# A hybrid attention and mLSTM block: where the identity matrix comes from, the order of the first loads, the place of the key transposes, and the order of some weight and activation forms

## The reference

```python
h = rms_norm(x, g_mix)
p = h @ w_in                       # columns: aq, ak, av, mq, mk, mv, mo, mi, mf
att = sliding_window_attention(rms_norm(aq), rms_norm(ak), av, sinks, slopes)   # 8 heads on 2 key heads
mq, mk = split(silu(causal_dwconv(concat(mq, mk))))
mh  = sigmoid(mo) * mlstm_chunkwise(mq, mk, mv, i_pre=mi, f_pre=mf)             # 4 heads
x = x + concat(rms_norm(att, g_att), rms_norm(mh, g_ml)) @ w_out
h2 = rms_norm(x, g_ffn)
x = x + (silu(h2 @ w_gate) * (h2 @ w_up)) @ w_down                              # D_FF = 2816
```

## Time and profile before

| | us |
|---|---|
| three timed runs | 1024.15, 1022.7, 1023.62 (median 1023.62) |
| the profiled execution, its own time | 1022.94 |
| its span, first to last instruction | 1021.1 |

### The profile page before, as it was taken

One profiled execution on the slowest core, in us unless ns is written; L12 is line 12 of the kernel. 1 busy time (PEld: TensorE's weight loads), 2 busy tenths in 40 slices (PEclk: granted clock), 3 DMA queues, 4 the chain that ended last, 5 costly groups with the idle time before them and its releaser, 6 DMA issues.

```text
span 1021.1 us, 13479 instructions
## 1 busy us (share of the span) xinstructions
PE 1005.1 (98%) x4970; PEld 831.3 (81%) x4970; DVE 646.9 (63%) x775; ACT 442.5 (43%) x912; POOL 691.5 (68%) x543
## 2 busy tenths in 40 slices
PE   9999999999999999999999999999999999999998
PEld 7898788877877887778888888888888888888886
DVE  4259426648862579584857676574848676574585
ACT  7555135547840558433434252433434252433440
POOL 0128768826566514988778688688778688688792
PEclk9999999999999999999999999999999999999999
DMA  7213202140131002111211211211211211211213
GB/s 228 68 53 91 77 28 67 60 154 22 32 110 57 25 18 82 52 42 42 83 42 42 83 42 42 82 42 42 83 42 42 83 42 42 83 41 43 84 58 136
DMA packets 71161, 66.06 MB, mean 65 GB/s; under 512 B 5304, under 2 KB 53688, under 8 KB 71096
## 3 DMA queue, kind: packets, MB, share of 16 engines
q1 hardware_dynamic: 70104, 64.71, 20.4%
q10 hardware_dynamic: 992, 0.49, 0.2%
HBM read 60.48 MB, written 4.21 MB: 63 GB/s over the span
## 4 chain that ended last, share of the span: by engine, by line
PE 91%; DVE 4%; issue 2%; ACT 2%; POOL 1%; DMA 0%; SPq 0%; DVEq 0%; POOLq 0%; ACTq 0%
PE banks L795 29%; PE banks L797 28%; PE banks L796 28%; PE banks L815 1%; ACT prob L1489 1%; PE banks L989 1%; PE banks L886 1%; DVE af_lo L2030 1%; PE banks L964 1%; POOL wr_raw L725 0%; PE banks L898 0%; DMA w_raw<-in_w_in 0%; PE banks L953 0%; PE banks L908 0%; PE banks L862 0%
## 5 line engine op out<-in xcount | busy, mean ns | idle before, releaser
L731 POOL TENSOR_TENSOR wr_lo<-wr_raw,wr_hi 128x512 fp32r<-128x512 f32 x231 | 318.8, 1412 | 26.8 <-ACT wr_hi L1309 21.7
L725 POOL TENSOR_TENSOR wr_raw<-wr_raw,wr_raw 128x512 f32<-128x512 f32 x132 | 193.8, 1473 | 138.0 <-PE banks L797 105.9
L795 PE MATMUL banks<-hf_hi,wr_hi 128*128 128x512 f32 x616 | 240.8, 391 | 1.8 <-DVE sg L2006 1.1
L797 PE MATMUL banks<-hf_hi,wr_lo 128*128 128x512 f32 x616 | 240.4, 390 | 0.0
L796 PE MATMUL banks<-hf_lo,wr_hi 128*128 128x512 f32 x616 | 240.1, 390 | 0.0
L1309 ACT ACTIVATE wr_hi<-wr_raw 128x512 fp32r<-128x512 f32 x231 | 136.7, 625 | 158.9 <-POOL wr_raw L725 100.4
L2109 DVE TENSOR_TENSOR x<-banks,x 128x1024 f32<-128x1024 f32 x138 | 168.8, 1224 | 53.3 <-PE banks L797 39.4
L795 PE MATMUL banks<-w_hi,actT_hi 128*128 128x512 f32 (+1 forms) x448 | 173.3, 387 | 0.9 <-DVE w_lo L1700 0.9
L797 PE MATMUL banks<-w_hi,actT_lo 128*128 128x512 f32 (+1 forms) x448 | 168.2, 376 | 0.0
L796 PE MATMUL banks<-w_lo,actT_hi 128*128 128x512 f32 (+1 forms) x448 | 167.8, 375 | 0.0
L795 PEld LDWEIGHTS banks<-hf_hi,wr_hi 128*128 128x128 f32 x616 | 115.6, 188 | 27.4 <-DVE sg L2006 2.0
(11 more groups left out here) (202 smaller groups left out, 1197.0 us busy)
## 6 DMA issues: line engine op xcount, KB each, us to landing
wr_raw<-in_w_up SPq DMA_DIRECT2D x46, 256.0 KB, 3.3
wr_raw<-in_w_gate SPq DMA_DIRECT2D x44, 256.0 KB, 3.4
wr_raw<-in_w_down SPq DMA_DIRECT2D x44, 256.0 KB, 3.1
w_raw<-in_w_in SPq DMA_DIRECT2D x32, 256.0 KB, 3.5
w_raw<-in_w_out SPq DMA_DIRECT2D x16, 256.0 KB, 2.7
x<-in_x SPq DMA_DIRECT2D x8, 512.0 KB, 6.4
out<-x SPq DMA_DIRECT2D x16, 256.0 KB, 2.1
x_in<-in_x SPq DMA_DIRECT2D x7, 512.0 KB, 4.0
```

The lines of the kernel that those rows point to most:

```text
L725: nc.gpsimd.tensor_tensor(wr_raw[slot(q, f)][:, :], wr_raw[slot(q, a)][:, :], wr_raw[slot(q, b)][:, :], ALU.subtract).then_inc(wsum, 1)
L731: nc.gpsimd.tensor_tensor(wr_lo[s][:, :], wr_raw[s][:, :], wr_hi[s][:, :].bitcast(F32), ALU.subtract).then_inc(wf_lo, 1)
L795: nc.tensor.matmul(ps, x_hi, wh, start=first, stop=False, skip_group_check=more)
L797: return nc.tensor.matmul(ps, x_lo, wh, start=False, stop=last, skip_group_check=more)
```

## The change

In seven places:

1. `ident` is not loaded any more. GpSimd makes it from the tile of ones with two `affine_select` instructions of 128x128, and TensorE waits for `ident_set`.
2. SP issues the first half of x first, then weight block 0, then the second half of x, then the other blocks; `grow` is issued by ScalarE. TensorE warms with 4 and 2 matmuls in place of 6 and 5, and transposes `grow` ahead of the tile. ScalarE does weight blocks 0 to 2 ahead of `high_bank(0, 1)` (before 0 and 1), VectorE blocks 0 to 3 ahead of `low_bank(0, 1)` (before 0 and 1).
3. `lf` is made before the keys are scaled; TensorE sums it after unit 18, and transposes the keys a unit later, after `u`; the copies to `kT` move with them.
4. On GpSimd, up 0's weight (q = 1): sums 5, 6, 4, then low part 6, then sum 7 and the other low parts; before: sums 5, 6, 7, 4 and then all low parts. The counts that ScalarE's `weight_high` waits for follow.
5. On VectorE in `first_gate_up`, `form_low(4)` is cut into two halves, and the add that frees the bank of gate 0 stands between them; TensorE waits for the second half only at its third k.
6. On VectorE in gate 1 (j = 1), the low part of form 3 moves behind the first add on bank 4, beside that of form 4.
7. The constants lose the identity's columns.

```diff
-            sp.dma_start(ident[:, :], consts[:, C_ID:C_ID + P]).then_inc(ident_s, 16)
             sp.dma_start(x_in[0][:, 0:N], x_t[0][:, 0:N]).then_inc(x_half_s, 16)
-            sp.dma_start(x_in[0][:, N:D], x_t[0][:, N:D]).then_inc(x_in_s[0], 16)
-            sp.dma_start(grow[:, :], g_mix.rearrange("a (k p) -> (a k) p", p=P)).then_inc(gmix_s, 16)
             for k in range(K):
                 sp.dma_start(w0_raw[:, k, :], w_in_k[k, :, MQ:MQ + N]).then_inc(w0_s[k], 16)
+                if k == 0:
+                    sp.dma_start(x_in[0][:, N:D], x_t[0][:, N:D]).then_inc(x_in_s[0], 16)
...
+            pool.wait_ge(ones_set, 1)
+            nc.gpsimd.affine_select(out=ident[:, :], in_=ones[:, :], pattern=[[1, P]], compare_op=ALU.is_ge,
+                                    fill=0.0, base=0, channel_multiplier=-1).then_inc(ident_lower, 1)
+            pool.wait_ge(ident_lower, 1)
+            nc.gpsimd.affine_select(out=ident[:, :], in_=ident[:, :], pattern=[[-1, P]], compare_op=ALU.is_ge,
+                                    fill=0.0, base=0, channel_multiplier=1).then_inc(ident_set, 1)
...
             pe.wait_ge(ones_set, 1)
-            keep_warm(6)
-            pe.wait_ge(ident_s, 16)
-            transpose_tile(x_in, 0, h_tp)
+            keep_warm(4)
+            pe.wait_ge(ident_set, 1)
             pe.wait_ge(gmix_s, 16)
             nc.tensor.transpose(bank[4][:, 0:K], grow[:, :], ident[0:K, 0:K]).then_inc(mix_tp, 1)
-            keep_warm(5)
+            transpose_tile(x_in, 0, h_tp)
+            keep_warm(2)
...
                 if U == 2 * T + 2:
-                    pe.wait_ge(kn_ready, 1)
-                    for b in range(2):
-                        for j in range(4):
-                            last = nc.tensor.transpose(bank[2 + b][:, j * P:(j + 1) * P],
-                                                       kvs[:, 4 * b + j, 2 * MH:2 * MH + KV * HD], ident[:, :])
-                    last.then_inc(kT_tp, 1)
-
                     pe.wait_ge(lf_ready, 1)
...
                 if U == 2 * T + 3:
                     pe.wait_ge(u_ready, 1)
                     nc.tensor.transpose(bank[6][0:32, 0:P], u_col[:, :], ident[:, :]).then_inc(uT_tp, 1)
+                    pe.wait_ge(kn_ready, 1)
+                    (the same eight transposes)
...
+            act.dma_start(grow[:, :], g_mix.rearrange("a (k p) -> (a k) p", p=P)).then_inc(gmix_s, 16)
             nc.scalar.preload_act_table_set("natural_log_exp_and_others")
             high_bank(0, 0, h_tp, h_hi)
             act.wait_ge(mix_ready, 1)
-            w0_high(0)
-            w0_high(1)
+            for k in range(3):
+                w0_high(k)
             high_bank(0, 1, h_tp, h_hi)
...
             low_bank(0, 0, h_hi, h_split)
-            w0_low(0)
-            w0_low(1)
+            for k in range(4):
+                w0_low(k)
             low_bank(0, 1, h_hi, h_split)
...
                     block_sum(q, 5, 7, 5)
+                    pool.wait_ge(wsum, sum_count(q, 5))
+                    pool.wait_ge(b22_s[q % 2], n)
+                    block_sum(q, 6, 3, 5)
+                    pool.wait_ge(wsum, sum_count(q, 6))
+                    pool.wait_ge(b21_again, 16)
+                    block_sum(q, 4, 4, 6)
+                    pool.wait_ge(wsum, sum_count(q, 4))
+                    block_low(q, 6)
+                    block_sum(q, 7, 3, 7)
+                    pool.wait_ge(wsum, sum_count(q, 7))
+                    for f in FORMS[3:]:
+                        block_low(q, f)
...
-                half_product(gate, 0, 4, False)
+                half_product(gate, 0, 4, False, second_half=8)
...
+                early = len(FORMS) - (2 if j == 1 else 1)
                 if j >= 1:
-                    for f in FORMS[1:-1]:
+                    for f in FORMS[1:early]:
                         act_low(j - 1, f)
                 dve.wait_ge(copied, 3 * g + 3)
                 add_product(sg[4], bank[4], 7 * g + 5)
                 if j >= 1:
-                    act_low(j - 1, FORMS[-1])
+                    for f in FORMS[early:]:
+                        act_low(j - 1, f)
...
-                form_low(4, slice(0, 4 * P), 7)
+                form_low(4, slice(0, 4 * P), 7, slice(0, 2))
                 dve.wait_ge(copied, copy_of(0, 2))
                 add_product(sg[4], bank[4], product(0, 7))
+                form_low(4, slice(0, 4 * P), 7, slice(2, 4))
```

More of the change, by code:

```diff
@@ L761, in _ @@
                     block_low(q, 2)
-                pool.wait_ge(wsum, 4 * q + 4)
-                for f in FORMS[2:]:
-                    block_low(q, f)
+                    for f in FORMS[2:]:
+                        block_low(q, f)
             for q in (QA, QB):
@@ L1060, in _ @@
                     nc.tensor.transpose(bank[6][0:32, 0:P], u_col[:, :], ident[:, :]).then_inc(uT_tp, 1)
+                    pe.wait_ge(kn_ready, 1)
+                    for b in range(2):
+                        for j in range(4):
+                            last = nc.tensor.transpose(bank[2 + b][:, j * P:(j + 1) * P],
+                                                       kvs[:, 4 * b + j, 2 * MH:2 * MH + KV * HD], ident[:, :])
+                    last.then_inc(kT_tp, 1)
                 if U == 2 * T + 4:
@@ L1107, in half_product @@
                 for k in range(4):
+                    if k == 2 and second_half:
+                        pe.wait_ge(h2_flo, second_half)
                     if k == 2 and tile is not None:
@@ L1329, in _ @@
             act.wait_ge(mix_ready, 1)
-            w0_high(0)
-            w0_high(1)
+            for k in range(3):
+                w0_high(k)
             high_bank(0, 1, h_tp, h_hi)
-            for k in range(2, K):
+            for k in range(3, K):
                 w0_high(k)
@@ L1710, in _ @@
             low_bank(0, 0, h_hi, h_split)
-            w0_low(0)
-            w0_low(1)
+            for k in range(4):
+                w0_low(k)
             low_bank(0, 1, h_hi, h_split)
-            for k in range(2, K):
+            for k in range(4, K):
                 w0_low(k)
@@ L1777, in _ @@
                 if U == 2 * T + 1:
+                    dve.wait_ge(softplus_done, 1)
+                    V_.scalar_tensor_tensor(lf[:, :].rearrange("p (t h) -> p t h", h=MH), fpre, 0.0,
+                                            expf[:, :].rearrange("p (t h) -> p t h", h=MH),
+                                            ALU.min, ALU.subtract).then_inc(lf_ready, 1)
                     dve.wait_ge(kv_rs, 1)
@@ L1807, in _ @@
                     V_.tensor_scalar(diag[:, :], tril32, cm[:, P - 1:P], None, ALU.mult).then_inc(umax_ready, 1)
+                    dve.wait_ge(kT_tp, 1)
+                    for b in range(2):
+                        step(V_.tensor_scalar(kT[:, CHUNK + b * N:CHUNK + (b + 1) * N], bank[2 + b][:, :],
+                                              cols[:, G_K:G_K + 1], None, ALU.mult))
                 if U == 2 * T + 4:
```

35 lines of the change are left out of this document (12 added, 23 removed).

## The result

| | before | after |
|---|---|---|
| timed runs, four each | 1022.70 to 1025.51, median 1023.88 | 1017.39 to 1018.04, median 1017.79 |
| ratio | | 0.9939, 95% interval 0.9922 to 0.9956 |
| the profiled execution, its own time | 1022.94 | 1017.68 |
| its span | 1021.1 | 1016.0 |

The change makes the kernel 0.6% faster. The runs of before spread over 2.8 us, those of after over 0.65; the experiments show that this is part of the result. The two profiled executions differ by 5.26 us, the forecast's terms made 3.9.

A forecast was written before the change was run, and what follows sets the result against it. TensorE, busy 1005.1 of 1021.1 us, was taken as the bound. Gains 1.45 + 0.95 + 1.0 + 0.5 = 3.9 took 1022.94 to 1019.0, or 1019.7 with the median's offset; predicted 1019.5, range 1017.9 to 1021.4.

The forecast's parts named there:

- the signs under "right": No TensorE idle over 0.2 at lf, seam forms 4 and 6, gate 1's form 4; affine_select by 3 us; unit 1 0.5 earlier.
- A pause costs the idle time shown plus 0.16: Price of each TensorE pause, from 512-column matmuls that start 0.23 us apart and show 0.39 each; four pauses, together 3.79.
- Keys: After unit 18 TensorE asks only for lf, ready near 102.7, and transposes the keys later: gain 1.45 us, bounds 1.0 and 1.53.
- Seam: Waits before 405.20 and 408.91 go, 0.44 + 0.81, less 0.3 given back by ScalarE's queue: gain 0.95, bounds 0.3 and 1.25.
- Rival 1: Seam: ScalarE's high part 7 waits for a late sum 7 and gives the 0.95 back: 1020.4 us; chance 0.13.
- Gate 1: A low part moves behind the add, which ends near 438.7, wanted at 439.39: gain 1.0 us, bounds 0.5 and 1.01.
- Start: Loads are issued earlier and the identity is hidden behind x: gain 0.5 us, bounds 0 and 0.83.
- the end of unit 0 follows those: Start: ScalarE takes the last three weight blocks as they land, so those landings set when unit 0 ends.
- Rival 2: The start gains nothing because transfers pace the landings: 1020.0 us; chance 0.08.
- rival 4: GpSimd's first affine_select is late and holds up unit 0; 4 us beyond 1.2 of free delay gives 1023; chance 0.06.
- Rival 5: TensorE's clock rises late at the start, 5.5 us a unit at half clock, two whole units low: 1027 us; chance 0.04.
- Rival 3: After unit 18, lf is late behind GpSimd by 0.5 or more: 1020.0 to 1020.4 us; chance 0.06.

The follow-up runs named there:

- the second measurement: The whole change measured once more on one chip beside a version with further edits: median 1018.19 us at full clock, ratio 0.9948 to the kernel before.
- keys_only: Only item 3 (lf made first, key transposes a unit later) put into the kernel before: 1021.22 us at full clock against 1022.88, ratio 0.9979.
- seam_only: Only items 4 and 5 (GpSimd's order for up 0, VectorE's form 4 cut) put into the kernel before: 1022.73 us at full clock against 1022.88, ratio 0.9997.
- start_only: Only items 1, 2 and 7 (identity on GpSimd, orders at the start) put into the kernel before: 1021.96 us at full clock against 1022.88, ratio 0.9991.
- grow_only: The kernel before with only the load of `grow` moved to ScalarE's queue: 1022.36 us at full clock against 1022.88, ratio 0.9991.
- gate_late: The kernel before, with form 4's low part in gate 1 also put ahead of the add on bank 4: 1024.17 us at full clock, ratio 1.0029.

## Why the prediction was off

**The direction and the mechanism of the keys, the seam and gate 1 were right; the sizes, the base and the start's path were not.** Pauses of TensorE were removed, and most of the gain came there. Of the signs under "right", 0.25 of idle stays at form 4 of gate 1, and unit 1 came 0.9 and not 0.5 earlier. The miss of 1.7 is 0.5 of base and 1.3 of terms that were priced too low or not at all, less 0.1 by which the median stands above the profiled execution. The upper bounds of the four terms add up to 4.6 (1.53, 1.25, 1.01, 0.83), below the 5.26 measured, so no choice within them would have met it. That the time lies outside the range at all is a matter of a tenth: the second measurement, 1018.19, lies inside.

**The base.** The forecast took the profiled execution's 1022.94 less 3.9, and moved up from 1019.0 to 1019.5 because the median of the timed runs stood higher. That half microsecond went the wrong way: 23 of 87 runs of before have the lower mean clock and are 2.7 above the others, and none of 70 with item 6 has it. So these runs do not remain as an offset, they are part of the gain. The prediction named this drift itself among the places where it fails most easily.

**"A pause costs the idle time shown plus 0.16"** was too little: the step behind the first matmul is 0.12 longer too. With 0.28 for each pause (0.24 for the one before 408.91, where the next step is 0.31) the rows of before give 1.66 for the keys (1.38 of idle), 1.45 for the seam (0.28 and 0.65) and, with 0.25 of idle left, 0.60 for gate 1: the measured 1.71, 1.48 and 0.61.

**Keys: 1.45 forecast, 1.71 measured, 1.66 in the runs of keys_only.** The mechanism is as written, and only the pause's price was off.

**Seam: 0.95 forecast, 1.48 measured in the whole change, 1.28 on top of gate 1's order.** The step that failed is the 0.3 that ScalarE's queue was to give back. High part 7 came about as late as forecast: it starts at 405.50, which with the 3.1 gained ahead of the seam is 408.6 on the clock of before, for 408.8. But from there to the copy ScalarE took 3.62, where the forecast had 4.0 (4.22 less 0.2 of pause), and the copy was done 0.3 before form 7. Rival 1 did not come.

**Gate 1: 1.0 forecast, 0.61 measured.** The step that failed is that the add ends near 438.7 and TensorE wants it at 439.39, with 0.7 of cover. Both times are from the timeline of before. With the seam's 0.95, by the forecast's own sum, TensorE wants it 0.95 earlier, and if VectorE's chain stays the cover is -0.25 and not 0.7. On the clock of before (3.1 added) TensorE wanted it at 437.9, 1.5 earlier than forecast, and the add ended at 438.3, only 0.4 earlier; the trace shows 0.25 of idle, and that it is the same figure is luck. The same slip in the reasoning hid the larger fact: the seam's term was worth next to nothing without gate 1's, as seam_only shows. The prediction added terms that were not independent, and was saved by the fact that both were in the change.

**Start: 0.5 forecast, 0.92 measured between the two profiles and in start_only's runs at full clock.** The bound was 0.83. The step that failed is "the end of unit 0 follows those", the landings. In the change's own profile no row of TensorE in unit 0 waits for a weight block, and the last low part ends 0.31 ahead of its matmul; in start_only's it is 1.26. What is earlier is unit 0's first matmul: 7.50 in the mean of the five profiles with the change's start, 8.47 in the seven with the old one, and slow steps have taken the place of waits. How the 0.92 is made up stays open. The last landing did move, by 1.3 in the mean of the profiles, more than the issues (0.83); 0.5 to 0.8 of that is `grow`, by one profile each. The forecast weighed the Trainium skill's page "Trainium Kernel Development and Optimization", section Key Constraints, by which issuing from a second queue saves issue time only, and took it to speak for less. In grow_only the last block landed 0.8 earlier than the mean of the old start for an issue 0.4 earlier; one profile against a spread of 1.0, so the rule is not refuted, but it gave no reason to shade the term. Rival 2 (nothing) falls. So does rival 4: the first `affine_select` began at 1.17 and took 0.29. The six microseconds of the Trainium skill's page "GPSIMD Engine Reference", section Instruction dispatch, do not show here; no row says whether its code was freshly loaded. (By the rival's own terms they would have cost 6 less 1.2, which is 4.8 and not some 4.)

**Rival 5, the clock at the start, came in part.** It was given 0.04 as a loss of several microseconds over whole units. It came as three slow steps here and up to nine in other profiles of the change's start, 0.2 each; in start_only the last of them ends at 11.45, so its sign, 0.43 and more behind 10 us, was seen there. It is not the new start's alone: seam_only and gate_late, with the old one, have four and three. The weight blocks hide only a part of it: where the change's start has five to nine of them, the last low part is done 1.1 to 1.4 early. Rival 3 did not come: `lf` took 0.80 and was 0.5 early.

**The mLSTM stretch's 0.40** was in no term. It belongs to the identity's source, by nine profiles against ten; how is open. The attention part's 0.09 was in none either and has no experiment.

## What to carry to other kernels

Price edits along the path one after the other: an edit that brings the bounding engine forward shortens the cover of every later hand-over whose other side does not move with it, so ask at each for the side that stays. Two edits can be worth nothing and 1.0 alone and 2.2 together. When timed runs of one kernel spread, look for a hand-over that can slip by a whole instruction of another engine; a change that shortens that pause removes the spread too, and the median gains more than the profile.

## What the runs showed of the hardware

A VectorE instruction of 128x512 with both inputs in SBUF took 0.69 us in two profiles and 1.75 to 1.85 in the other 17, started at most 0.1 from one of GpSimd's in all of them; TensorE's pause in gate 1 was 0.85 where it took 0.69, and 1.92 to 2.29 where it took longer and item 6 or gate_late's edit was not in. Behind pauses of 1.92, 1.94, 2.29 and 3.96 us the granted clock fell for six to eight steps from matmul to matmul (0.72 in a window of seam_only), behind another of 2.29 and behind those of about 1.5 in the attention part it did not. At the start the 512-column matmuls ran 0.43 apart, as at the lower level, in windows whose granted clock is printed as 1.00: there the step between matmuls tells more than that column.
